# A two-block transformer layer on one core: heads turned and first scores inside the last projection group, probabilities turned a step sooner, four w_out chunks ahead of the second turn

## The reference

```
h = rms_norm(x, attn_norm)
mq, mk, mv, dq, dk, dv = split(h @ w_in)                  # six groups of 512 columns
a_out = moba_attention(rope(norm(mq)), rope(norm(mk)), mv)  # 8 heads of 64
b_out = diff_attention(rope(norm(dq)), rope(norm(dk)), dv)  # 4 heads: (A1 - lam*A2) V
x = x + concat(norm(a_out), norm(b_out)) @ w_out
x = x + peer_ffn(rms_norm(x, ffn_norm), ...)              # 256 gathers of expert rows
... second block: mixer, attention over a memory (keys from w_xkv), MLP
```

## Time and profile before

| what | value |
|---|---|
| median of 3 runs | 1402.89 us (1401.67 to 1402.97) |
| the profiled execution | 1401.84 us |
| its span in the trace | 1400.0 us |
| mean granted TensorE clock | 0.966 of full |
| PE, POOL, DVE, ACT busy | 1250.1, 887.4, 812.8, 612.2 us |

### The profile page before, as it was taken

The page is one execution under the profiler, slowest core; times in us unless marked ns, Lnnn a source line. Parts: engine busy times, 40 slices in busy tenths (PEclk is TensorE's granted clock), DMA queues, the critical chain, the costliest instruction groups (busy, mean ns, idle before and its releaser), DMA issues.

```text
span 1400.0 us, 17652 instructions
## 1 busy us (share of the span) xinstructions
PE 1250.1 (89%) x5974; PEld 887.6 (63%) x5974; DVE 812.8 (58%) x1575; ACT 612.2 (44%) x1296; POOL 887.4 (63%) x533
## 2 busy tenths in 40 slices
PE   7999999888988987677787898999999999999997
PEld 6878785444444533233333344799999988899886
DVE  5934397777877677877667654603652632277301
ACT  5566434334443442322333323447455345555432
POOL 5633766555766645544544451996868964799985
PEclk9999999999999998899999899999999999999999
DMA  7532489999999999999999996464636633455652
GB/s 264 182 104 75 166 316 389 425 427 425 417 426 426 424 427 426 427 426 428 428 426 419 419 427 273 145 207 133 188 126 201 206 123 121 137 194 182 208 195 92
DMA packets 72943, 400.69 MB, mean 286 GB/s; under 512 B 8096, under 2 KB 8352, under 8 KB 39712
## 3 DMA queue, kind: packets, MB, share of 16 engines
q0 software_dynamic: 36864, 268.45, 45.8%
q1 hardware_dynamic: 33696, 123.35, 27.1%
q10 hardware_dynamic: 2304, 7.85, 1.5%
HBM read 396.48 MB, written 3.15 MB: 285 GB/s over the span
## 4 chain that ended last, share of the span: by engine, by line
PE 35%; DMA 21%; issue 16%; POOL 15%; DVE 7%; ACT 4%; POOLq 0%; ACTq 0%; SPq 0%; DVEq 0%
DMA arena<-in_experts,arena 21%; POOL w_lo L1413 12%; PE bank L896 9%; PE bank L600 8%; PE bank L602 7%; PE bank L601 7%; DVE arena L1778 4%; POOL arena L1464 3%; PE bank L653 1%; ACT arena L1224 1%; ACT diag L1230 1%; DMA ring<-in_stream 1%; PE bank L662 0%; DVE arena L1718 0%; ACT arena L1063 0%
## 5 line engine op out<-in xcount | busy, mean ns | idle before, releaser
L1413 POOL TENSOR_TENSOR w_lo<-ring,w_hi 128x1024 fp32r<-128x1024 f32 x222 | 560.9, 2549 | 183.6 <-ACT w_hi L1050 182.7
L896 PE MATMUL bank<-arena,diag 128*128 128x512 f32 x968 | 459.0, 626 | 90.9 <-ACT diag L1230 90.9
L1464 POOL DMA_INDIRECT arena<-in_experts,arena x242 | 287.0, 1186 | 244.3 <-PE bank L896 184.2
L1778 DVE CUSTOM_DVE_ANT_0 arena<-arena 128x1024 f32<-128x1024 f32 x242 | 318.9, 1331 | 163.5 <-DMA arena<-in_experts,arena 163.3
L896 PEld LDWEIGHTS bank<-arena,diag 128*128 128x128 f32 x968 | 187.0, 199 | 342.4 <-issue 206.7
L1050 ACT ACTIVATE w_hi<-ring 128x1024 fp32r<-128x1024 f32 x228 | 240.0, 1058 | 175.2 <-PE bank L602 121.6
L600 PE MATMUL bank<-hT_hi,w_hi 128*128 128x256 f32 x736 | 210.4, 286 | 5.8 <-DVE hT_lo L1499 2.7
L602 PE MATMUL bank<-hT_hi,w_lo 128*128 128x256 f32 x736 | 206.4, 280 | 0.0
L601 PE MATMUL bank<-hT_lo,w_hi 128*128 128x256 f32 x736 | 206.2, 280 | 0.0
L1221 ACT ACTIVATE arena<-arena 128x2 f32<-128x2 f32 (+2 forms) x99 | 20.2, 204 | 408.5 <-DVE arena L1778 408.3
L600 PEld LDWEIGHTS bank<-hT_hi,w_hi 128*128 128x128 f32 x736 | 139.1, 189 | 11.6 <-issue 10.3
(11 more groups left out here) (251 smaller groups left out, 1673.2 us busy)
## 6 DMA issues: line engine op xcount, KB each, us to landing
ring<-in_stream SPq DMA_DIRECT2D x228, 512.0 KB, 3.6
arena<-in_experts,arena POOLq DMA_INDIRECT x242, 14.7
kv_park<-arena ACTq DMA_DIRECT2D x8, 256.0 KB, 7.7
arena<-kv_park ACTq DMA_DIRECT2D x1, 2048.0 KB, 7.7
x_res<-in_x SPq DMA_DIRECT2D x2, 512.0 KB, 5.4
arena<-in_mem SPq DMA_DIRECT2D x1, 1024.0 KB, 11.4
arena<-in_sub_keys ACTq DMA_DIRECT2D x1, 1024.0 KB, 6.5
out<-arena SPq DMA_DIRECT2D x2, 512.0 KB, 2.6
```

The costliest lines, as they stand in the source:

```text
L896: mm = pe.matmul(y_banks[half][:, :], diag[:, slot % DIAGS, :], rows_buf[BUFFER[slot]][:, D + 512 * half:D + 512 * half + 512], start=(i = ...
L1413: nc.gpsimd.tensor_tensor(w_lo[:, slot, :], ring[:, slot, :], w_hi[:, slot, :].bitcast(F32), ALU.subtract).then_inc(S("lo_made"), 1)
L1464: nc.gpsimd.indirect_dma_start(out=rows_buf[b], out_offset=None, in_=experts, in_offset=bass.IndirectOffsetOnAxis(ap=expert_u[:, slot:slot ...
L1778: v.tensor_tensor_reduce(out=rows_buf[b][:, 0:D], in0=xn[:, slot // (PEER_H * PEER_K), :], in1=rows_buf[b][:, 0:D], scale=1.0, scalar=0.0, ...
```

## The change

TensorE turns the first four halves of q and k after the second of the last projection group's four chunks, and forms the two score maps of the first unit after the third chunk, the map of the second unit behind the fourth. Six results get banks of their own (`EARLY_BANK`), since the projection holds others. Four fillers before the first score go; every score map from step 2 on gets one filler (13 maps). The probabilities of a unit are turned two steps after its scores (three before), ahead of the memory pieces; ACT copies them two of its own steps after the exponentials (one before), and DVE takes pv four steps after (three before). With this DVE's multiply of the differential heads moves from step 13 to step 12, its sum from step 10 to 11, ACT's squares from step 9 to 10. ACT copies the last value group after the first unit's exponentials. Four chunks of `w_out`, not two, come before the second `turn_mix`.

```
     for step in range(12 + 4):                 # plan(): scores of steps 0 and 1 stand ahead of the loop
...
-        if 3 <= step < 15:
-            add(("pT", HEAD_ORDER[step - 3]))
+        if 2 <= step < 14:
+            add(("pT", HEAD_ORDER[step - 2]))
...
+    for g, half in TURN_ORDER[:4]:
+        place, chunk, results, _ = table["qkT", g, half]
+        table["qkT", g, half] = (place, chunk, results, LAST["w_in"] - 3)
...
-PLAIN_TURNED = 2
+PLAIN_TURNED = 4
+EARLY_BANK = {("qkT", 2, 0): 1, ("qkT", 3, 0): 2, ("qkT", 0, 0): 3, ("qkT", 1, 0): 5, ("score", 8): 6, ("score", 9): 7}
...
@@ TensorE @@
-            for n in range(6):
+            for n in range(5):
                 natural("w_in", 4, n, h_, FIRST["w_in"], normed("attn") if n == 0 else None)
...
-            pe.wait_ge(S("roped"), 4)
-            turn_heads(TURN_ORDER[:4])
...
+            def among_values(i):
+
+                if i == 2:
+                    pe.wait_ge(S("roped"), 4)
+                    turn_heads(TURN_ORDER[:4])
+                elif i == 3:
+                    for m in maps_of(HEAD_ORDER[0]):
+                        score(m)
+
+            natural("w_in", 4, 5, h_, FIRST["w_in"], among_values)
+            for m in maps_of(HEAD_ORDER[1]):
+                score(m)
...
             for step in range(16):
                 if step == 5:
                     turn_heads(TURN_ORDER[6:])
-                if step < 12:
+                if 2 <= step < 12:
                     for m in maps_of(HEAD_ORDER[step]):
-                        score(m, 4 if step == 0 and m == MAP_ORDER[0] else 0)
+                        score(m, 1)
                 if step == 1:
                     norm("mem", memn)
                     turn_heads(TURN_ORDER[4:6])
+                if 2 <= step < 14:
+                    turn_probs(HEAD_ORDER[step - 2], 2 if step >= 12 else 0)
                 if step in KEY_PIECES:
...
-                if 3 <= step < 15:
-                    turn_probs(HEAD_ORDER[step - 3], 2 if step >= 12 else 0)
@@ ScalarE @@
-            for step in range(13):
+            for step in range(14):
                 if step < 12:
                     for m in maps_of(HEAD_ORDER[step]):
                         exps(m)
+                if step == 0:
+                    for t in range(TT):
+                        values_out(5, t)
...
-                if step == 6:
+                if step == 7:
                     park([(("xk", 0), None)], "xk", 0)
-                if step == 9:
+                if step == 10:
                     att_square(range(8, 12), slice(512, 1024))
-                if step >= 1:
-                    u = HEAD_ORDER[step - 1]
+                if step >= 2:
+                    u = HEAD_ORDER[step - 2]
                     if u not in TURNED_BY_DVE:
                         copy_out(("pT", u), pT[:, u, :], n=SC)
@@ VectorE @@
-                if step == 10:
+                if step == 11:
                     dve.wait_ge(S("att_squares"), 1)
...
-                if step == 13:
+                if step == 12:
                     dve.wait_ge(S("att_rstd"), 1)
...
-                if step >= 3:
-                    u = HEAD_ORDER[step - 3]
+                if step >= 4:
+                    u = HEAD_ORDER[step - 4]
                     bank = take(dve, ("pv", u))
```

More of the change, by code:

```diff
@@ L156, in plan @@
         add(("qkT", g, half))
+    for step in range(2):
+        for m in maps_of(HEAD_ORDER[step]):
+            add(("score", m))
     for step in range(12 + 4):
@@ L264, in plan @@
                 bank = KEY_BANK + key[1]
+            elif key in EARLY_BANK:
+                bank = EARLY_BANK[key]
             else:
@@ L1116, in _, with values_out @@
             norm_out("attn", con("g_attn"))
-            for n in range(6):
+            def values_out(n, t):
+                act.wait_ge(S("rstd"), 2 * seq["attn"] + t + 1)
+                copy_out(("w_in", n, t), proj1[n][:, t, :], rstd["attn"][:, t:t + 1])
+            for n in range(5):
                 for t in range(TT):
@@ L1123, in _ @@
                           .then_inc(S("squares"), 1)
-                    else:
-                        act.wait_ge(S("rstd"), 2 * seq["attn"] + t + 1)
-                        copy_out(("w_in", n, t), proj1[n][:, t, :], rstd["attn"][:, t:t + 1])
+                    elif n == 4:
+                        values_out(n, t)
                 if n < 4:
@@ L1630, in mix_lo @@
                 split_lo(("mixT", g), [hT_1[k] for k in ks], [ghead[:, k:k + 1] for k in ks])
-            for step in range(12 + 3):
+            for step in range(12 + 4):
                 if step < 12:
```

## The result

The changed kernel took 1418.36 us (median of 4 runs, 1414.30 to 1419.77) against 1402.28 of the kernel before on the same chip: ratio 1.0121, 95% interval 1.0097 to 1.0144. It is slower, by more than I forecast: 1418.36 lies 9.9 us above my 1408.5 and 5.9 us above the top of my range, 1412.5. Two later measurements of the same kernel gave 1.0119 (1.0098 to 1.0139) and 1.0095 (1.0071 to 1.0119), that is +13 to +17 us. The profiled execution took 1419.77 us.

The account below looks back on a forecast made before the run. TensorE's stretch to w_out's first product was to bound: 54.0 work + 3.05 + 0.5 + 3.5 waits + 3.2 clock = 64.3 against 59.7 us, +4.5; with w_out's 1.7, +6.2 on 1402.3 gives 1408.5 us, range 1401.5 to 1412.5.

Parts of the forecast that it names:

- the three waits: New TensorE waits: for the last value group's copies (3.05 us), the last probabilities (3.5) and inside w_out (1.7).
- Work: TensorE's work from projection end to w_out's first product: 50.8 us plus seven fillers at 0.45 each, 54.0 us.
- First new wait: Behind the third score, before the memory's norm: TensorE waits 3.05 us for ACT's copies of the last value group.
- The 0.5 us behind it: After the memory's transposes, TensorE waits 0.5 us for a bank for step 2's score, until their split.
- In the loop: Attention steps up to step 10: the old 1.3 us wait for a score bank goes, no new one comes.
- Second new wait: Before the last pv: TensorE waits 3.5 us for head 7's copy, behind DVE's multiply and POOL's root.
- so I take DVE: At the last probabilities: DVE's multiply, not POOL's lo part of chunk 31, starts first; otherwise 2.4 us later.
- Third: In w_out behind the second turn: TensorE waits 1.7 us for DVE's lo parts of the group just turned.
- The clock: Behind the two long waits: a shorter 1.2 GHz piece of 1.6 us loss each, 3.2 us together.
- 5.0 lost to the clock: Kernel before, projection end to w_out: two profiled 1.2 GHz pieces cost 5.0 of 59.7 us.
- does not reach the end of the kernel unchanged: Behind w_out: a shift there was taken to reach the kernel's end unchanged; otherwise the forecast is wrong.
- POOL first on the port: Rival, chance 0.10: at the last probabilities POOL's lo part starts before DVE's multiply, 2.4 us more, 1410.9 us.

Follow-up runs that it names:

- e6: The changed kernel without the 13 fillers in the scores; ratio 1.0059 to the kernel before.
- e5: The changed kernel with ACT making the hi parts of chunks 24 and 25 ahead of the copies of q and k; ratio 1.0076 to the kernel before.
- e16: The changed kernel measured again without any edit, beside kernels with pure delays; ratio 1.0095 to the kernel before.
- e2: The changed kernel with POOL making the lo part of chunk 31 only after DVE's multiply; ratio 1.0090 to the kernel before.
- e4: The changed kernel with two w_out chunks ahead of the second turn again, instead of four; ratio 1.0088 to the kernel before.
- e1: The changed kernel with DVE's multiply of the differential heads back in step 13, behind the copy of head 7; ratio 1.0085 to the kernel before.
- e10: The changed kernel with the edits of e1, e4 and e5 together; ratio 1.0043 to the kernel before.
- e11: The kernel of e10, also without the 13 fillers between the scores; ratio 1.0001 to the kernel before, 1400.05 us.
- e8: The kernel before with 25 more fillers on TensorE ahead of w_out, a pure delay; ratio 1.0086 to the kernel before.
- e12: The kernel of e11 with POOL's root ahead of the lo parts of chunks 30 and 31, these behind DVE's multiply; ratio 0.9980 to the kernel before, 1397.35 us.

## Why the prediction was wrong

The sign was right, and so were the three waits and what ends them. Two terms of the sum were too small by 2.3 us each: the second wait, because POOL and not DVE went first, and the clock. A third thing was taken for fixed that is not: the profile that all was counted from. Of the 9.9 us between 1408.5 and 1418.36, 5.1 lie before the end of w_out (+11.3 instead of +6.2) and the rest behind it.

- **Work.** Right to 0.6 us: 54.0 of work + 3.2 + 5.8 of waits + 5.5 of clock makes 68.5 us, and 150.42 - 81.30 = 69.1 were measured. The price of 0.45 for a filler was too low for those between the two maps of one unit (e6). Against the kernel before this counts for one unit only, since there one of the two pairs of maps in question was already split by the wait of 1.3 us.
- **First new wait** 3.05: measured 3.17, for the named copies (ACT makes three hi parts from 83.72 on, then the copies). Right; e5 shows the cause. **The 0.5 us behind it** did not come in this trace, in which TensorE's transposes ran at half clock and lasted as long as the split; in e5 and e16, where the clock was higher, 0.4 us came.
- **In the loop** no wait to 137.5 us. Right. e6 shows beyond it that the fillers there kept nothing up.
- **Second new wait** 3.5: measured 5.75. Root and TensorE were in their forecast places to 0.2 us; the failed step is "so I take DVE". I had priced the other outcome at 2.4 us and given it 0.10; it came in all three traces of the changed kernel (3.28 us each) and in the seven others in which the same root releases both, POOL 0.07 to 0.14 us ahead; e2 took the 2.1 us away. One meeting in which DVE had been first was no ground for DVE: there POOL's lo part waited for ACT, here both were released by one root. That POOL wins because it made the root itself fits these ten traces, but is argued only.
- **Third** 1.7: measured 1.6 as a wait and 1.9 as w_out's longer time; e4 takes back 1.6. Right.
- **The clock** 3.2: measured 5.5. The failed step is "I take the shorter piece ... once behind each of the two long waits". The two pieces took 2.9 and 2.6. The second came in all eight traces in which TensorE stood before the last pv, for 3.4 to 6.1 us (0.86 in the last column); behind the waits of 3.0 and 3.5 us for the turn (e1, e10, e11) it lasted half as long, 0.93. The first came behind every wait of 3.2 us, shorter in six traces (0.89) and longer in two (0.79).
- **The baseline.** The "5.0 lost to the clock" was read from one execution as a property of the kernel before. In three of six traces it is 0, so the kernel before is on average better in this stretch than its one profile. First turns at 138.28, 138.19, 136.41, 134.73, 134.60 and 134.84 us have a mean of 136.2, 2.1 us before the profile's. The changed kernel's delay at the end of w_out is on that count 11.3 + 2.1 = 13.4 us, and the three ratios say 13 to 17; its own traces hardly differ there (175.43 to 175.65). Behind w_out the same trace is off the other way: from the second marker to the end it takes 1235.6 us, and every other trace, of either order, takes longer, 1237.1 to 1243.8. Between 1100 and 1260 us alone the other seventeen are 1.3 to 4.2 us slower than it. In its whole time the two nearly cancel, but a marker counted from it does not say what the ratio says: 4.0 of e11's missing 6 us and 1.8 of e8's 3.3 are steps behind w_out against this trace.
- **The way to the end.** A shift that "does not reach the end of the kernel unchanged" I had named as what would make it wrong. It went from +11.3 to +18.0 in the first trace, 4.5 of it at the convolution (+11.2 at 1005 us, +15.7 at 1030 by the products of before), to +13.8 and +12.5 in the others. The five other traces of the old order show such steps too, 1.6 to 4.2 us, so much of the surplus is the quick profile of before. What decides in one execution which engine is first at the convolution, and why that profile was quick between 1100 and 1260 us, is not settled.

Of the rivals "POOL first on the port" came true, together with the forecast; as an alternative to it, at 1410.9, it was still 7.5 us short: 2.3 of that is the clock, most of the rest came behind w_out.

## What to carry to other kernels

Where two engines are released by the same instruction and can exclude each other, price the sum with the worse order, and look whether the instruction with slack can be put behind. Price what stands behind a waiting instruction on its queue: here a copy of 0.54 us behind a multiply made a wait of 3.0 us into one of 5.8, since the work that could have filled the wait waited too. Look where a filler stands: between two products that would run side by side it costs more than its length. A clock piece in one profile is a draw, and so is the time of any later stretch: take a second trace of the unchanged kernel before counting what a change may win back or lose.

## What was not expected of the hardware

- Waits of 1.3 and 1.5 us were followed by 1.2 GHz in some executions and not in others, of the same instructions (0, 3.5 or 5 us lost in six traces). In e12 a piece came behind waits of 0.8, 0.4 and 0.2 us (0.89 from 84 to 100 us); e11 has the same three waits and none. Behind the waits of 3.4 to 6.1 us before the last pv it came in eight of eight.
- From 100 to 128 us the granted clock was 1.0 in all twelve traces of the changed order, with and without its 13 filler products.
- The sixteen transposes that began in the slow piece took 3.65 us, 1.9 times the 1.94 of the earlier trace rows; DVE's multiply took 3.28 us beside POOL's lo part against 1.22 alone; the 2.06 between them are nearly all of a lo part (2.34).
- Nine more filler products ahead of w_out, 3.5 us of work, moved the first product of w_out by 0.0 us between two traces: the spread of the clock was as large as the edit.
- Two maps whose operands lie in different halves of the partitions took 0.87 us side by side, as long as one map; with a filler between them 2.33 us.
